# Five merges of one branch among the recurrence's chunks, none right behind its scores

## The chip, the cores and the metric

The kernel runs on one core of a Trainium2 chip. Its engines are TensorE (PE, with its weight loads as PEld), VectorE (DVE), ScalarE (ACT), GpSimd (POOL) and SyncE (SP, which issues the transfers). The metric is the device time of one execution in microseconds; lower is better.

## The reference

Two blocks on 256 tokens of width 1024. The first is a mixer and a mixture of experts; the second is two layers of feed-forward and attention. Only the mixer matters here:

```
proj = x @ w_in
y_a = rg_lru(...)                    # branch 0
y_b = gated_delta_rule(...)          # branch 1
y_c = stick_breaking_attention(...)  # branch 2
y_d = gla_chunked(...)               # branch 3
gates = sigmoid(merge_in)            # 4 x 1024 columns of proj
merged = sum over n of gates[:, :, n] * (y_n @ w_branch[n])
out = merged @ w_out
```

The recurrence of branch 3, with 16 chunks of 16 tokens and 4 heads:

```
attn = where(causal, q_dec @ k_inv.T, 0);  o_intra = attn @ v
def step(state, xs):
    o_i = q_i @ state
    state = state * gl_i[..., :, None] + kd_i.T @ v_i
    return state, o_i
```

## The kernel before

All four branches run on one core, and what stands in the list STEPS sets the order of the work on PE, ACT and DVE: each engine walks the same list and does its own part of each step. Weights come in units of 1 MB into a ring of six slots; SP requests a unit as soon as the slot that it needs is free.

A merge step ("merge", k) makes 128 of the 1024 output columns of one branch. PE does eight fp32 matmuls of 256 columns for the gate (xT times a unit of w_in) and four for the branch (yT times a unit of w_branch). In the trace each fp32 matmul is two instructions, so a merge reads as x16 and x8. ACT takes the sigmoid (sg), DVE multiplies and adds to merged (two operations of 0.42 us). There are 32: 0 to 7 for branch 0, 8 to 15 for branch 2 (the second in BRANCH_ORDER, attention), 16 to 23 for branch 3, 24 to 31 for branch 1. A merge needs only its branch's finished yT, a ring unit and one of two PSUM banks, so it can stand among steps of another branch. Merges 3, 7, 11 and so on free three ring slots.

The steps of branch 3 around the change:

- d_attn: PE makes the scores (gl_q, gl_k) and transposes d_kd. DVE masks the scores into d_at and makes two masked copies of the transposes, d_kn, 1.3 us each.
- d_intra: PE multiplies d_at with gl_v. It waits for both copies.
- d_chunk c: PE makes the chunk's update (d_kn times gl_v, four matmuls of 128 columns on 32 rows), DVE adds it to the decayed state in four operations (d_B in the trace), PE then reads out chunk c with the state that DVE wrote for the chunk before (gl_q with d_B, four matmuls of 16 columns).
- d_end: ACT squares the result, PE sums (d_e with ones, two matmuls of 512 columns), ACT makes the norm in two steps with table loads, DVE scales and gates into yT.
- b_rows: PE starts the next branch (rowbc with ones). It waits for DVE's yT of d_end.

_weave puts a list of merges evenly among a list of steps, the first one behind the first step. The waits on PE that matter, of d_chunk, d_intra and b_rows (comments mine):

```
pe.wait_ge(sem("d_S"), c)      # the read-out waits for DVE's state
t.see("d_am")                  # d_intra waits for the masked copies
pe.wait_ge(sem("y3"), 1)       # b_rows waits for yT of branch 3
```

Of the kernel before, what the change touches and what calls it, by code (L numbers as in the profile page):

```python
# [70 lines left out]
STEPS = [("proj", w, u) for w in "abcd" for u in range(PROJ_UNITS[w])]  # L71
# [19 lines left out]
def _weave(steps, tiles):  # L91
    out, put = [], 0
    for n, s in enumerate(steps):
        out.append(s)
        while put < len(tiles) and put * len(steps) < (n + 1) * len(tiles):
            out.append(tiles[put])
            put += 1
    return out + tiles[put:]


_MERGE = [("merge", k) for k in range(4 * DT)]
for hp in range(4):
    STEPS += [("c_z", hp), _MERGE[2 * hp], ("c_cum", hp), _MERGE[2 * hp + 1], ("c_out", hp)]
STEPS += [("d_gate",), ("b_pre",), _MERGE[8], _MERGE[9], ("d_attn",), _MERGE[10], ("d_intra",)]
STEPS += _weave([("d_chunk", c) for c in range(16)], _MERGE[11:14])
STEPS += [("d_end",), _MERGE[14], _MERGE[15], ("b_rows",), ("b_decay",), _MERGE[16], _MERGE[17], ("b_kk",), _MERGE[18],
          ("b_nat",), _MERGE[19]]
STEPS += _weave([(s, lv, half) for lv in range(1, 6) for s in ("b_y", "b_xy") for half in range(2)]
                + [("b_uw",)] + [(s, c) for c in range(4) for s in ("b_w", "b_o")] + [("b_end",)],
# [2520 lines left out]
```

## Time and profile before

| | us |
|---|---|
| median of 3 runs | 2322.02 |
| the three runs | 2322.02, 2322.64, 2316.07 |
| the profiled execution | 2322.17 |
| its span | 2320.4 |

The profiled execution's own time is 1.8 us above its span. Over the span PE is busy for 90%, DVE for 51%, ACT for 40%. The page's line of the granted clock gives TensorE's clock in tenths of full speed; its mean is 0.923. There are two levels, 1.00 (2.4 GHz) and 0.50 (1.2 GHz). The steps that the change touches lie between 330 and 430 us.

### The profile page before, as it was taken

The page shows a single profiled execution, that of the slowest core. Times are in us where ns is not written, and L with a number is a line of the kernel's source. Part 1 is how long each engine was busy: PE and PEld are TensorE (multiplying, and loading weights), DVE is VectorE, ACT ScalarE, POOL GpSimd, SP SyncE. Part 2 cuts the span into 40 slices and gives each one's busy share as a digit, 9 for nine tenths or more (in the row PEclk, how much of TensorE's full clock was granted, in tenths as well). Part 3 has the DMA queues.
Part 4 walks back from the last instruction along what each step waited for, and adds up shares of the span by engine and source line. Part 5 has one row for each costly group of instructions (what it writes and reads, how often), then busy time and mean ns, then how long its engine had stood idle before and what let it go on. Part 6 is the DMA issues. An engine that isn't in the chain of part 4 may idle for free.

```text
span 2320.4 us, 29178 instructions
## 1 busy us (share of the span) xinstructions
PE 2079.5 (90%) x11729; PEld 1722.8 (74%) x11729; DVE 1193.4 (51%) x1737; ACT 932.4 (40%) x1341; POOL 52.0 (2%) x126
## 2 busy tenths in 40 slices
PE   8999879989998999996899877879989998658998
PEld 6777668778467878775899752379989988536998
DVE  2060243441177878888555545455565555344554
ACT  1232530211045766675434523433354345344433
POOL 5000000000000000000000000000000000000000
PEclk9999886988989999998999998989999998759999
DMA  7775111203587888886365579335555555203553
GB/s 229 272 263 172 55 55 55 85 25 120 220 327 268 319 308 310 290 329 249 127 198 175 171 291 398 123 122 190 183 182 164 182 172 189 92 0 127 179 187 105
DMA packets 205351, 435.49 MB, mean 188 GB/s; under 512 B 7744, under 2 KB 158368, under 8 KB 181696
## 3 DMA queue, kind: packets, MB, share of 16 engines
q1 hardware_dynamic: 201568, 424.70, 52.7%
q0 software_dynamic: 3680, 9.37, 1.2%
q8 instruction: 70, 1.15, 0.2%
q14 instruction: 33, 0.27, 0.0%
HBM read 432.85 MB, written 1.20 MB: 187 GB/s over the span
## 4 chain that ended last, share of the span: by engine, by line
PE 62%; DVE 8%; ACT 5%; DMA 2%; issue 2%; DVEq 0%; ACTq 0%; SPq 0%
PE P L642 60%; ACT big L1419 2%; DMA ring<-in_ada_w 1%; DVE w_lo L2306 1%; DMA ring<-in_w_up 1%; DVE w_lo L1909 1%; ACT merged L1419 1%; DVE xs L1858 1%; PE P L1257 0%; PE P L658 0%; DVE big L1858 0%; DVE st L2494 0%; ACT xT L1419 0%; DVE xT L1854 0%; ACT w_hi L1455 0%
## 5 line engine op out<-in xcount | busy, mean ns | idle before, releaser
L1909 DVE TENSOR_TENSOR w_lo<-ring,w_hi 128x1024 fp32r<-128x1024 f32 x302 | 351.7, 1220 | 96.4 <-ACT w_hi L1455 96.2
L642 PE MATMUL P<-x_hi,w_hi 128*128 128x256 f32 x1280 | 362.9, 284 | 6.0 <-DVE w_lo L1909 6.0
L642 PE MATMUL P<-x_hi,w_lo 128*128 128x256 f32 x1280 | 363.5, 284 | 0.0
L642 PE MATMUL P<-x_lo,w_hi 128*128 128x256 f32 x1280 | 360.8, 282 | 0.0
L1455 ACT ACTIVATE w_hi<-ring 128x1024 fp32r<-128x1024 f32 x302 | 297.5, 1050 | 65.1 <-DMA ring<-in_ffn_w_down 62.3
L2306 DVE TENSOR_TENSOR w_lo<-ring,w_hi 128x1024 fp32r<-128x1024 f32 x240 | 279.2, 1221 | 22.1 <-ACT w_hi L1644 20.3
L642 PE MATMUL P<-w_hi,x_hi 128*128 128x256 f32 (+2 forms) x752 | 259.1, 345 | 24.9 <-DVE x_lo L1851 15.1
L1644 ACT ACTIVATE w_hi<-ring 128x1024 fp32r<-128x1024 f32 x240 | 240.4, 1053 | 100.6 <-DMA ring<-in_w_up 40.0
L642 PE MATMUL P<-xT,ring 128*128 128x256 f32 x1152 | 271.7, 394 | 3.1 <-ACT xT L1419 3.1
L642 PEld LDWEIGHTS P<-xT,ring 128*128 128x128 f32 x1152 | 225.9, 199 | 50.1 <-issue 18.1
L642 PE MATMUL P<-w_lo,x_hi 128*128 128x256 f32 (+2 forms) x752 | 256.8, 341 | 0.0
L642 PE MATMUL P<-w_hi,x_lo 128*128 128x256 f32 (+2 forms) x752 | 253.6, 337 | 0.0
L642 PEld LDWEIGHTS P<-x_hi,w_hi 128*128 128x128 f32 x1280 | 243.3, 190 | 10.0 <-DVE w_lo L1909 6.7
L642 PEld LDWEIGHTS P<-x_lo,w_hi 128*128 128x128 f32 x1280 | 244.9, 191 | 2.8
L642 PEld LDWEIGHTS P<-x_hi,w_lo 128*128 128x128 f32 x1280 | 244.3, 191 | 0.0
L642 PE MATMUL P<-w_hi,hid_hi 128*128 128x512 f32 x512 | 203.7, 398 | 4.7 <-DVE w_lo L2306 4.4
L642 PE MATMUL P<-w_lo,hid_hi 128*128 128x512 f32 x512 | 205.1, 401 | 0.0
L642 PE MATMUL P<-w_hi,hid_lo 128*128 128x512 f32 x512 | 201.5, 394 | 0.0
L1635 ACT ACTIVATE silu<-P 128x256 f32<-128x256 f32 x88 | 33.9, 385 | 372.9 <-PE P L642 356.4
L642 PEld LDWEIGHTS P<-w_hi,x_hi 128*128 128x128 f32 x752 | 149.9, 199 | 43.2 <-issue 19.7
L2286 DVE TENSOR_TENSOR hid<-silu,P 128x256 f32<-128x256 f32 (+1 forms) x80 | 33.7, 422 | 263.7 <-ACT silu L1635 263.1
L642 PEld LDWEIGHTS P<-w_hi,x_lo 128*128 128x128 f32 x752 | 149.2, 198 | 14.7
(437 smaller groups left out, 2472.0 us busy)
## 6 DMA issues: line engine op xcount, KB each, us to landing
ring<-in_ada_w SPq DMA_DIRECT2D x72, 1024.0 KB, 9.4
ring<-in_ffn_w_gate SPq DMA_DIRECT2D x44, 1024.0 KB, 5.5
ring<-in_ffn_w_up SPq DMA_DIRECT2D x44, 1024.0 KB, 7.9
ring<-in_ffn_w_down SPq DMA_DIRECT2D x44, 1024.0 KB, 4.9
ring<-in_w_in SPq DMA_DIRECT2D x40, 1024.0 KB, 7.4
ring<-in_w_gate SPq DMA_DIRECT2D x40, 1024.0 KB, 5.0
ring<-in_w_up SPq DMA_DIRECT2D x40, 1024.0 KB, 5.0
ring<-in_w_down SPq DMA_DIRECT2D x40, 1024.0 KB, 5.1
```

The costliest lines, as they stand in the source:

```text
L642: return pe.matmul(o, l, r, start=start, stop=stop, **kw)
L1419: a.done(act.activation(o, i, fn, **kw), name)
L1455: act.activation(w_hi[:, slot, c:c + half], ring[:, slot, c:c + half], ACT.Copy).then_inc(sem("w_hi"), 1)
L1635: act.activation(silu[:, k % 2, :], P[:, k % 2, 0:S], ACT.Silu).then_inc(sem("silu"), 1)
L1644: act.activation(w_hi[:, n % R, c:c + UNIT // 2], ring[:, n % R, c:c + UNIT // 2], ACT.Copy).then_inc(sem("w_hi"), 1)
L1858: v.done(dve.scalar_tensor_tensor(out=o, in0=x, scalar=s, in1=y, op0=op0, op1=op1), name)
L1909: dve.tensor_tensor(w_lo[:, slot, c:c + half], ring[:, slot, c:c + half], w_hi[:, slot, c:c + half].bitcast(F32), ALU.subtract).then_inc(s ...
L2286: dve.tensor_tensor(x, silu[done:128, k % 2, :], P[done:128, k % 2, S:2 * S], ALU.mult).then_inc(sem("hid_part"), 1)
L2306: dve.tensor_tensor(w_lo[:, n % R, c:c + UNIT // 2], ring[:, n % R, c:c + UNIT // 2], w_hi[:, n % R, c:c + UNIT // 2].bitcast(F32), ALU.su ...
```

## The change

Merge 10 no longer stands between d_attn and d_intra, and merge 14 no longer stands behind d_end. Both go into the recurrence, so that five merges (10 to 14) lie among its 16 chunks where there were three (11 to 13). Nothing else is changed.

```
-STEPS += [("d_gate",), ("b_pre",), _MERGE[8], _MERGE[9], ("d_attn",), _MERGE[10], ("d_intra",)]
-STEPS += _weave([("d_chunk", c) for c in range(16)], _MERGE[11:14])
-STEPS += [("d_end",), _MERGE[14], _MERGE[15], ("b_rows",), ("b_decay",), _MERGE[16], _MERGE[17], ("b_kk",), _MERGE[18],
+STEPS += [("d_gate",), ("b_pre",), _MERGE[8], _MERGE[9], ("d_attn",), ("d_intra",)]
+STEPS += _weave([("d_chunk", c) for c in range(16)], _MERGE[10:15])
+STEPS += [("d_end",), _MERGE[15], ("b_rows",), ("b_decay",), _MERGE[16], _MERGE[17], ("b_kk",), _MERGE[18],
```

On PE, from the scores on (L807 is the transpose, xT and yT with ring are the two halves of a merge, d_at with gl_v is d_intra, d_kn with gl_v is the update of chunk 0):

```order
 L642 MATMUL P<-gl_q,gl_k 128x128 x8
 L807 MATMUL P<-ident,d_kd 128x128 x8
-L642 MATMUL P<-xT,ring 128x256 x8
-L642 MATMUL P<-yT,ring 128x256 x4
 L642 MATMUL P<-d_at,gl_v 128x128 x8
 L642 MATMUL P<-gl_v,d_kn 128x128 x4
 L642 MATMUL P<-xT,ring 128x256 x8
 L642 MATMUL P<-yT,ring 128x256 x4
```

The merge between transposes and d_intra is gone; the merge behind chunk 0 stays in its place (it was merge 11 and is now merge 10).

On PE in the changed kernel, from the read-out of one chunk over a merge and three chunks to the next merge (gl_v with d_kn is a chunk's update, gl_q with d_B its read-out):

```order
L642 MATMUL P<-gl_q,d_B 128x16 x4
L642 MATMUL P<-xT,ring 128x256 x8
L642 MATMUL P<-yT,ring 128x256 x4
L642 MATMUL P<-gl_v,d_kn 128x128 x4
L642 MATMUL P<-gl_q,d_B 128x16 x4
L642 MATMUL P<-gl_v,d_kn 128x128 x4
L642 MATMUL P<-gl_q,d_B 128x16 x4
L642 MATMUL P<-gl_v,d_kn 128x128 x4
L642 MATMUL P<-gl_q,d_B 128x16 x4
L642 MATMUL P<-xT,ring 128x256 x8
L642 MATMUL P<-yT,ring 128x256 x4
```

Three chunks stand between two merges, where five stood before: the merges come behind chunks 0, 3, 6, 9 and 12, not 0, 5 and 10.

On PE at the end of the recurrence (d_e with ones are the sums of d_end):

```order
 L642 MATMUL P<-gl_v,d_kn 128x128 x4
 L642 MATMUL P<-gl_q,d_B 128x16 x8
 L642 MATMUL P<-d_e,ones 128x512 x2
-L642 MATMUL P<-xT,ring 128x256 x8
-L642 MATMUL P<-yT,ring 128x256 x4
 L642 MATMUL P<-xT,ring 128x256 x8
 L642 MATMUL P<-yT,ring 128x256 x4
```

One merge is left between the sums and b_rows. ACT's and DVE's parts of the merges move in the same way; POOL's and SP's lists are the same.

## Rows read from the trace of the kernel before

**Rows 1.** The page: busy time by engine, and one DMA row.
```profile
PE 2079.5 (90%) x11729; PEld 1722.8 (74%) x11729; DVE 1193.4 (51%) x1737; ACT 932.4 (40%) x1341; POOL 52.0 (2%) x126
...
ring<-in_w_in SPq DMA_DIRECT2D x40, 1024.0 KB, 7.4
```

**Rows 2.** Timeline, 330 to 343 us: start, length, engine, line, operation, operands, count.
```profile
333.60 1.91 PE L807 MATMUL P<-ident,d_kd 128*128 128x128 f32 x8
...
335.30 3.66 PE L642 MATMUL P<-xT,ring 128*128 128x256 f32 x16
335.62 2.60 DVE L1855 TENSOR_SCALAR d_kn<-P,parity 128x1024 f32<-128x1024 f32 x2
...
340.52 1.95 PE L642 MATMUL P<-d_at,gl_v 128*128 128x128 f32 x16
...
342.40 1.15 PE L642 MATMUL P<-gl_v,d_kn 32*128 32x128 f32 x8
```

**Rows 3.** Timeline, 343 to 364 us: first merge in the recurrence.
```profile
343.49 3.72 PE L642 MATMUL P<-xT,ring 128*128 128x256 f32 x16
...
348.86 1.15 PE L642 MATMUL P<-gl_v,d_kn 32*128 32x128 f32 x8
...
350.49 1.50 DVE L1858 SCALAR_TENSOR_TENSOR d_B<-d_B,d_gl,P 128x128 f32<-128x128 f32 x4
...
353.53 2.07 PE L642 MATMUL P<-gl_v,d_kn 32*128 32x128 f32 x8
...
357.35 2.07 PE L642 MATMUL P<-gl_v,d_kn 32*128 32x128 f32 x8
```

**Rows 4.** Timeline of PE, 364.85 to 409 us: second and third merge.
```profile
364.90 5.97 PE L642 MATMUL P<-xT,ring 128*128 128x256 f32 x16
...
372.53 1.15 PE L642 MATMUL P<-gl_v,d_kn 32*128 32x128 f32 x8
...
376.95 2.07 PE L642 MATMUL P<-gl_v,d_kn 32*128 32x128 f32 x8
...
388.32 6.20 PE L642 MATMUL P<-xT,ring 128*128 128x256 f32 x16
...
396.18 1.15 PE L642 MATMUL P<-gl_v,d_kn 32*128 32x128 f32 x8
...
400.37 2.07 PE L642 MATMUL P<-gl_v,d_kn 32*128 32x128 f32 x8
```

**Rows 5.** Windows, PE alone: stretch, length, busy (instructions), granted clock, DMA share, GB/s.
```profile
352.40:364.80 12.40, 12.40 (x55) 0.50 0.65 218
364.80:369.50 4.70, 4.70 (x13) 0.50 0.00 0
...
376.30:388.30 12.00, 12.00 (x53) 0.50 0.01 1
```

**Rows 6.** Timeline, 410 to 430 us: end of the recurrence.
```profile
410.97 3.41 PE L642 MATMUL P<-d_e,ones 128*128 128x512 f32 x4 [1.17 <-ACT d_e L1419]
...
414.22 3.62 PE L642 MATMUL P<-xT,ring 128*128 128x256 f32 x16
...
419.34 1.22 DVE L1851 TENSOR_TENSOR d_e<-d_e,P 128x1024 f32<-128x1024 f32 x1 [11.49 <-ACT d_e L1419]
...
420.60 1.28 DVE L1858 SCALAR_TENSOR_TENSOR yT<-d_e,cols,gate_d 128x1024 f32<-128x1024 f32 x1
...
424.58 3.60 PE L642 MATMUL P<-rowbc,ones 128*128 128x512 f32 x8
```

**Rows 7.** Timeline of PE, 454 to 475 us: two gaps, with their length in brackets.
```profile
459.42 1.16 PE L642 MATMUL P<-b_X,rowbc 128*128 128x128 f32 x8 [2.42 <-DVE rowbc L1851]
...
468.02 1.67 PE L642 MATMUL P<-b_X,rowbc 128*128 128x128 f32 x8 [2.26 <-DVEq L222]
```

**Rows 8.** Windows, PE alone: the same stretches.
```profile
457.00:465.00 8.00, 5.58 (x31) 1.00 0.76 258
468.50:471.90 3.40, 3.40 (x19) 0.50 0.02 8
```
## The prediction

> **What bounds the kernel now.** I read four views in this order: the page's busy times, the timeline around the moved merges, the windows with the granted clock, and the timeline again for the gaps further on. The page [rows 1] says that the tensor engine (PE) works for 90% of the span, so the question is always what PE does at a given place, and at which of its two clocks. The change touches about 95 us of 2320.
>
> Place one, behind the scores. The transposes end at 333.60 + 1.91 = 335.51. DVE then needs until 335.62 + 2.60 = 338.22 for the two masked copies (d_kn) that the intra step waits for. PE does not stand still, because merge 10 runs from 335.30 to 340.52, and the intra step follows at 340.52 [rows 2]. So merge 10 (5.2 us) covers a hole of some 2.8 us.
>
> Place two, the recurrence, from 342.40 [rows 2] to 410.97 - 1.17 = 409.80 [rows 6], with three merges in it. The reader would expect PE to wait for DVE there: each chunk's state update takes DVE 1.50 us and the next chunk's read needs it. The windows show otherwise: PE is busy all the time (12.40 of 12.40 us), but at half clock, 0.50, which is 1.2 GHz [rows 5]. A chunk takes 357.35 - 353.53 = 3.82 us at that clock [rows 3], while the first two behind a merge take 4.67 us together [rows 3], or 4.42 and 4.19 us [rows 4], so 2.1 us each at full clock. A merge that starts at full clock takes 348.86 - 343.49 = 5.37 us [rows 3]; one that starts at half clock takes 7.63 us (364.90 to 372.53) or 7.86 us (388.32 to 396.18) [rows 4]. What the engine did before the changes: the clock rose 4.7 us into a merge (at 369.5, of one that began at 364.8), and it was down again at 352.4 and 376.3, 3.5 and 3.8 us behind a merge's end, PE having been busy throughout with chunks [rows 3 to 5]. So merges raise the clock and chunks lose it, with a lag on both sides.
>
> Place three, behind the recurrence. The norm's sums start at 410.97; two merges follow from 414.22; b_rows starts at 424.58. b_rows needs yT of this branch, which DVE finishes at 420.60 + 1.28 = 421.88, 10.91 us behind the start of the sums [rows 6]. The two merges outlast that by 2.7 us, one merge would not.
>
> **The change part by part.** No instruction is added or removed on any engine, only rows move. The sum is made against the profiled execution, 2322.17 us.
>
> 1. Merge 10 leaves place one. The intra step then waits for DVE and starts at about 338.22 + 0.1 = 338.3 instead of 340.52: 2.2 us earlier. The merge's 5.2 us are not saved but paid inside the recurrence, so a hole of 2.8 us is uncovered. The intra step takes 342.40 - 340.52 = 1.88 us and chunk 0's first half 343.49 - 342.40 = 1.09 us [rows 2, 3], which ends at 341.3.
>
> 2. The recurrence now has merges behind chunks 0, 3, 6, 9 and 12. Merge 10 starts at full clock if that has held: 5.37, then two chunks 4.67, then the third at half clock 3.82, together 13.86 us, which gives 355.1. The next three groups start at half clock: a merge of 7.75 (mean of 7.63 and 7.86), two chunks of 4.30 (mean of 4.42 and 4.19), one of 3.82, together 15.87 us; three are 47.6, which gives 402.7. The last group has 7.75 + 4.30 and then only the reading half of chunk 15, a little under half of a slow chunk, 1.85: 13.9, which gives 416.6. Before it was 409.80: 6.8 us later. DVE's two small merge operations per merge come two times more, but behind a merge the update ran from 350.49 to 351.99 and the read that needs it, of chunk 2, follows PE's own work [rows 3]; I cost them at nothing. If they were not covered it would be under 1 us each.
>
> 3. Merge 14 leaves place three. The sums, ACT's steps and DVE's two steps stay as they are, so yT is ready 10.91 us behind the start of the sums and b_rows starts about 10.95 behind it, where it was 424.58 - 410.97 = 13.61 before: 2.65 us earlier. Merge 15 alone runs from 3.25 to 8.6 us behind the start, so a second hole of 2.3 us is uncovered in front of b_rows.
>
> 4. The holes can cost clock as well. Two gaps of PE of like length stand further on: 2.42 us before 459.42, with the clock at 1.00 all through, and 2.26 us before 468.02, with 0.50 from 468.5 to 471.9 [rows 7, 8]. So a fall is about an even matter, and it lasts 3.4 us, which costs half of that, 1.7. The bounds are 0 and 3.4 for the two holes together, and more if merge 10 begins at half clock, when it costs 7.75 instead of 5.37. I take 1.6.
>
> 5. Ring slots: merge 11's end frees three slots, and moves from about 349 to about 362. A transfer takes 7.4 us from its issue [rows 1], and the first reader is merge 16, behind b_rows, over 50 us later. No cost; the cover is the rest of the recurrence.
>
> Sum: 6.8 - 2.65 + 1.6 = +5.8 us, which makes 2328.0. The same from the other side: PE's work is the same, the two holes add 2.8 + 2.3 = 5.1 us of idle time, and the time at half clock stays nearly what it was, as five short slow stretches replace three long ones. The reason that more merges do not help is that three chunks at full clock last 6.2 us, longer than the 3.5 to 3.8 us after which the clock is gone. The median shown, 2322.02, is close to the profiled time, but one of the three runs is at 2316.07, so the moments at which the clock steps may well shift a run by several us.
>
> **Rivals.**
>
> *The clock holds* (faster). If three chunks between merges were few enough to keep 2.4 GHz, the recurrence would take 1.09 + 5 x 5.37 + 14 x 2.1 + 1.0 = 58.3 us from 340.2, ending at 398.5 instead of 409.8. With the sums at full clock (1.7 less) and place three's 2.65 that is 15.7 us less: 2306.5. Against it: both falls came within 4 us of a merge, with a busy PE [rows 4, 5]. The place that decides is the third chunk of each group.
> The Trainium skill, "TensorE: Matmul & The Clock Gate", section "What's actually happening", says that the clock is low by default and that activity releases it. If any busy PE counts as active, that page speaks for this rival. The trace disagrees with so plain a reading: PE was 12.00 of 12.00 us busy at 0.50 [rows 5].
>
> *The rises come early* (no change). The lag between a merge's start and the rise was 4.7 us, but nothing ties it to the merge. If the four later merges got their clock after about 2 us, each would cost some 1.3 us less: 5.8 - 5.2 = +0.6, so 2322.8. For it speaks that merges now follow the last rise more closely; against it, both merges seen at half clock cost almost the same [rows 4].
>
> *Both holes lose the clock* (slower still). PE stands for 2.8 us before the intra step, falls to 1.2 GHz, and intra, chunk 0 and merge 10's first part run at it: 1.9 + 1.1 us become twice as long and merge 10 takes 7.75, 5.4 us at most; b_rows adds 1.7. From the 4.2 of steps 1 to 3 that gives up to +11, and with the merge that follows recovering a part, about +9.5: 2331.7. The second gap of rows 7 speaks for it, the first against it.
>
> **How the numbers follow.** Forecast 0.45, clock holds 0.08, early rises 0.27, both holes 0.20. A measurement of this kernel can tell about 0.3%, that is 7 us, from no change. Faster by more comes only with the first rival: 0.08. Slower by more than 7 us (above 2329) takes the last rival, 0.20, and about a third of the forecast's own spread, which runs from 2324 to 2332: 0.36 in all. The rest, 0.56, is within 0.3%. The range reaches over the forecast and both rivals beside it, and down over half of the way to the first: 2315 to 2335.
>
> **What would show it.** In the changed trace: PE idle for about 2.8 us before the intra matmuls and about 2.3 us before b_rows; the clock at 0.50 in the third chunk of each group; the merges in the recurrence at 7.6 to 7.9 us but for the first; the recurrence's end 6 to 8 us later than 409.80, and merge 16's start 4 to 8 us later. Wrong would be: clock 1.00 across a whole group, merges of 5.4 us inside the recurrence, an intra step that waits for nothing, or a shift that is made up for later, for instance by a wait for a transfer that shrinks.

## The result and the profile after

| | before | after |
|---|---|---|
| median of 20 runs, us | 2316.64 | 2323.65 |
| lowest to highest, us | 2310.55 to 2322.64 | 2317.64 to 2328.83 |
| the profiled execution, us | 2322.17 | 2320.24 |
| its span, us | 2320.4 | 2318.5 |

The changed kernel is slower: the ratio of its runs to those of before is 1.0030, with a 95% interval of 1.0019 to 1.0041. Of 2316.64 us that is 7.0 us by the medians, and between 4.4 and 9.5 by the interval. The interval excludes 1, so the change is slower, but by hardly more than these runs can tell. The ratios here and below are worked out over the runs and can differ a little from the quotient of the two medians. One run of the kernel before in the second batch of experiments took 8225.72 us, counts as slow and is left out of the ratios.

The two profiled executions stand the other way round, 1.9 us apart. Each is one draw out of a spread of 11 to 12 us, so their spans do not compare the kernels. What can be compared is a stretch that starts and ends at the same instruction in both. I use the one from the start of the score matmuls (gl_q with gl_k) to the start of merge 16 (the first xT with ring behind b_rows): 330.02 to 429.62, 99.60 us, before; 324.61 to 429.69, 105.08 us, after. So within the traces the change costs 5.5 us, and what came before the scores had happened to be 5.4 us shorter.

The windows over the two stretches, before first (stretch, length, PE busy, granted clock, DMA share, GB/s), show where the 5.5 us are:

```profile
330.02:429.62 99.60, 98.43 (x453) 0.73 0.13 42
324.61:429.69 105.08, 99.62 (x453) 0.75 0.12 42
```

PE stands idle for 1.17 us before and for 5.46 us after, so 4.3 of the 5.5 us are idle time. The time at half clock, read in windows of 0.1 us, is 53.3 us before and 53.1 us after: two merges more among the chunks did not shorten it. The last 1.2 us are in PE's busy time and are not broken down further.

Place one in the changed kernel, in the timeline (start, length, engine, line, operation, operands, count; idle time before it in brackets). These rows answer to [rows 2]:

```profile
324.61 3.78 PE L642 MATMUL P<-gl_q,gl_k 128*128 128x128 f32 x16 [11.15 <-DVE gl_k L1851]
...
328.18 1.91 PE L807 MATMUL P<-ident,d_kd 128*128 128x128 f32 x8
...
330.20 2.60 DVE L1855 TENSOR_SCALAR d_kn<-P,parity 128x1024 f32<-128x1024 f32 x2
...
332.87 3.34 PE L642 MATMUL P<-d_at,gl_v 128*128 128x128 f32 x16 [2.77 <-DVE d_kn L1855]
...
336.14 1.46 PE L642 MATMUL P<-gl_v,d_kn 32*128 32x128 f32 x8
...
337.52 3.72 PE L642 MATMUL P<-xT,ring 128*128 128x256 f32 x16
```

PE stands for 2.77 us in front of the intra step, waiting for DVE's d_kn. The intra step then takes 336.14 - 332.87 = 3.27 us instead of 1.88. The clock was still at 1.00 through the idle time and fell at 333.4, 0.5 us into the step. From the scores' start to chunk 0's start it is 11.53 us where it was 342.40 - 330.02 = 12.38.

The recurrence, answering to [rows 3, 4]. Each pair is a merge's start and the start of the first chunk behind it; the rows of 2.07 us are third chunks:

```profile
342.90 1.15 PE L642 MATMUL P<-gl_v,d_kn 32*128 32x128 f32 x8
...
347.06 2.07 PE L642 MATMUL P<-gl_v,d_kn 32*128 32x128 f32 x8
...
350.79 5.21 PE L642 MATMUL P<-xT,ring 128*128 128x256 f32 x16
...
357.66 1.15 PE L642 MATMUL P<-gl_v,d_kn 32*128 32x128 f32 x8
...
362.71 2.07 PE L642 MATMUL P<-gl_v,d_kn 32*128 32x128 f32 x8
...
366.44 5.91 PE L642 MATMUL P<-xT,ring 128*128 128x256 f32 x16
...
374.01 1.15 PE L642 MATMUL P<-gl_v,d_kn 32*128 32x128 f32 x8
...
378.48 2.07 PE L642 MATMUL P<-gl_v,d_kn 32*128 32x128 f32 x8
...
382.21 6.55 PE L642 MATMUL P<-xT,ring 128*128 128x256 f32 x16
...
390.42 1.15 PE L642 MATMUL P<-gl_v,d_kn 32*128 32x128 f32 x8
...
398.10 5.45 PE L642 MATMUL P<-xT,ring 128*128 128x256 f32 x16
...
405.20 1.15 PE L642 MATMUL P<-gl_v,d_kn 32*128 32x128 f32 x8
```

The first merge takes 342.90 - 337.52 = 5.38 us, the others 6.87, 7.57, 8.21 and 7.10. The third chunks run at half clock (366.44 - 362.71 = 3.73). The windows show the clock, answering to [rows 5]:

```profile
333.50:336.70 3.20, 3.20 (x15) 0.50 0.00 0
350.80:353.70 2.90, 2.90 (x8) 0.50 0.00 0
366.40:370.80 4.40, 4.40 (x11) 0.50 0.57 181
382.20:387.90 5.70, 5.70 (x15) 0.50 0.00 0
```

The first is the intra step, the others are the first parts of merges 11, 12 and 13: PE is busy in all of them, at 1.2 GHz. The clock comes back 3.1 to 5.8 us into these merges. It is gone again by the start of the third chunk, in one group 0.2 us into it.

Place three, answering to [rows 6]:

```profile
413.14 3.78 PE L642 MATMUL P<-d_e,ones 128*128 128x512 f32 x4 [1.17 <-ACT d_e L1419]
...
416.71 4.61 PE L642 MATMUL P<-xT,ring 128*128 128x256 f32 x16
...
424.57 3.67 PE L642 MATMUL P<-rowbc,ones 128*128 128x512 f32 x8 [1.52 <-DVE yT L1858]
...
429.69 3.72 PE L642 MATMUL P<-xT,ring 128*128 128x256 f32 x16
```

The one merge left starts at half clock and takes longer, and b_rows waits another 1.52 us for yT. From the sums' start to merge 16's start it is 16.55 us, where it was 429.62 - 410.97 = 18.65.

### The profile page after: what moved, and what is told of

It reads as the page before. It is cut to its first block, busy times and chain, and to the rows that moved or that the text cites. A ratio compares the mean times of both kernels' runs of the same rounds, so it can differ in the third digit from the quotient of the medians.

```text
span 2318.5 us, 29178 instructions
## 1 busy us (share of the span) xinstructions
PE 2074.8 (89%) x11729; PEld 1719.0 (74%) x11729; DVE 1193.7 (51%) x1737; ACT 931.6 (40%) x1341; POOL 51.8 (2%) x126
## 4 chain that ended last, share of the span: by engine, by line
PE 62%; DVE 9%; ACT 5%; DMA 2%; issue 2%; DVEq 0%; ACTq 0%
PE P L642 60%; ACT big L1419 2%; DVE w_lo L2306 1%; DMA ring<-in_ada_w 1%; DMA ring<-in_w_up 1%; DVE w_lo L1909 1%; ACT merged L1419 1%; DVE xs L1858 1%; PE P L658 0%; PE P L1257 0%; DVE big L1858 0%; DVE st L2494 0%; ACT xT L1419 0%; DVE xT L1854 0%; ACT w_hi L1455 0%
## 5 line engine op out<-in xcount | busy, mean ns | idle before, releaser
L642 PE MATMUL P<-w_hi,x_hi 128*128 128x256 f32 (+2 forms) x752 | 260.2, 346 | 25.1 <-DVE x_lo L1851 15.1
```

Source lines behind the costliest of these rows:

```text
L642: return pe.matmul(o, l, r, start=start, stop=stop, **kw)
```

## The experiments

Every stretch below is read from one profiled execution. By my estimate it carries an error of 1 to 2 us from where the clock's steps fell: the same piece of work behind the recurrence took 18.65 us in one trace and 20.24 in another. Each kernel has 6 to 12 runs, against 11 to 33 runs of the kernel before in the same batch (medians 2318.47, 2319.36 and 2318.97 in the three batches). "The stretch" is from the scores to merge 16, 99.60 us before and 105.08 with the change. In the expectations, theory A is the prediction's account (idle time is uncovered, the time at half clock stays); rival B is another one, named anew for each kernel. "Recurrence" is from chunk 0's start to the end of the last read-out, which is 1.17 us in front of the sums.

**Each half of the change alone.**

```
# e1_first: merge 10 moved, 14 and 15 at the end
STEPS += [..., _MERGE[8], _MERGE[9], ("d_attn",), ("d_intra",)]
STEPS += _weave([("d_chunk", c) for c in range(16)], _MERGE[10:14])
STEPS += [("d_end",), _MERGE[14], _MERGE[15], ("b_rows",), ...]
# e2_second: merge 14 moved, 10 behind the scores
STEPS += [..., ("d_attn",), _MERGE[10], ("d_intra",)]
STEPS += _weave([("d_chunk", c) for c in range(16)], _MERGE[11:15])
STEPS += [("d_end",), _MERGE[15], ("b_rows",), ...]
```

> Only merge 10 is moved (from behind the scores into the recurrence, four merges there); merges 14 and 15 stay at the end. Measure: the stretch from the start of the score matmuls to the start of merge 16, 99.6 us before and 105.1 with the whole change. Theory A (two uncovered holes, time at half clock about conserved): the hole of 2.8 us in front of the intra step is there, b_rows has none; the stretch is 102 to 104 us, the median 2 to 5 us above before. Rival B (the loss comes from merges that start at half clock in the recurrence, not from the holes): the loss goes with the number of merges added there, so half of it, about 2.7 us, with the clock steady across the hole.

> Only merge 14 is moved (from behind the recurrence into it, four merges there); merge 10 stays behind the scores. Theory A: no hole in front of the intra step, one of 1.5 to 2.7 us in front of b_rows; stretch 101 to 102.5 us, median 1 to 3 us above before, less than with merge 10 moved alone. Rival B: the same 2.7 us as for merge 10 alone.

Measured: e1_first 2324.46 us, ratio 1.0017 (1.0002 to 1.0032); e2_second 2324.03 us, ratio 1.0021 (1.0002 to 1.0040). Both are slower, and their medians do not tell them apart. The medians are 6.0 and 5.6 us above before, more than the 2 to 5 and 1 to 3 us expected; the ratios make it 3.9 and 4.9 us, with intervals that reach down to 0.5 us. PE's timeline of e1_first (the starts of scores, intra step, chunk 0, sums, merge 14 and merge 16):

```profile
322.86 3.79 PE L642 MATMUL P<-gl_q,gl_k 128*128 128x128 f32 x16 [11.15 <-DVE gl_k L1851]
...
331.12 3.31 PE L642 MATMUL P<-d_at,gl_v 128*128 128x128 f32 x16 [2.77 <-DVE d_kn L1855]
334.36 1.48 PE L642 MATMUL P<-gl_v,d_kn 32*128 32x128 f32 x8
...
407.46 3.78 PE L642 MATMUL P<-d_e,ones 128*128 128x512 f32 x4 [1.17 <-ACT d_e L1419]
411.03 4.88 PE L642 MATMUL P<-xT,ring 128*128 128x256 f32 x16
...
427.70 3.72 PE L642 MATMUL P<-xT,ring 128*128 128x256 f32 x16
```

and of e2_second (scores, chunk 0, sums, b_rows, merge 16):

```profile
326.64 3.78 PE L642 MATMUL P<-gl_q,gl_k 128*128 128x128 f32 x16 [11.14 <-DVE gl_k L1851]
...
339.01 1.15 PE L642 MATMUL P<-gl_v,d_kn 32*128 32x128 f32 x8
...
411.91 3.78 PE L642 MATMUL P<-d_e,ones 128*128 128x512 f32 x4 [1.17 <-ACT d_e L1419]
...
423.34 3.67 PE L642 MATMUL P<-rowbc,ones 128*128 128x512 f32 x8 [1.60 <-DVE yT L1858]
...
428.45 3.72 PE L642 MATMUL P<-xT,ring 128*128 128x256 f32 x16
```

With merge 10 gone the same hole of 2.77 us and the same slow intra step are there; with merge 10 in its place the chunks begin 12.37 us behind the scores, as before. The recurrence takes 71.9 us (334.36 to 407.46 - 1.17) and 71.7 us with four merges. The stretches are 104.84 and 101.81 us. The second is as theory A had it, the first 0.8 us above its range. In the first, rival B has the clock steady across the hole, and it was not. The second, 2.2 us longer than before, does not tell A from B, which said 2.7.

The two losses, 5.2 and 2.2 us, make 7.4 together where the whole change has 5.5. Part of this is place three of e1_first: its merge 14 began at half clock (merge 15 at full), so it took 427.70 - 407.46 = 20.24 us against 18.65, for the same work. The clock came back 2.9 us behind the start of the sums in the trace of before, and 6.1 us behind it in this one. It came back 5.1 to 5.7 us behind it in after, e2_second, e3_fill, e4_block, e6_split3 and e8_none, and 3.3 in e7_early. So the trace of before is a favourable draw at this place. That moving merge 10 costs more than moving merge 14 is seen in these traces and not settled by the medians.

**The holes filled.**

```
+ for _ in range(5):      # before the wait of d_intra; 3 before that of b_rows
+     mm(P[:, 2, 0:S], xT[:, 0, 0:128], xT[:, 0, :])
```

> The changed kernel with extra matmuls of 256 columns on a free PSUM bank in both holes, five in front of the intra step and three in front of b_rows; their results are overwritten and no work is left out. They take no time that was not idle. Theory A: the clock stays at 1.00 through both holes, so intra and chunk 0 take 3.0 us as before instead of 4.65, and the stretch is 103 to 104 us where the change has 105.1: the idle time itself is not given back. If the holes cost nothing but clock, the stretch would be near 100.

Measured: 2324.97 us, ratio 1.0022 (1.0004 to 1.0040), not told from the changed kernel's 1.0030. Its trace:

```profile
330.44 3.79 PE L642 MATMUL P<-gl_q,gl_k 128*128 128x128 f32 x16 [11.15 <-DVE gl_k L1855]
...
338.70 2.05 PE L642 MATMUL P<-d_at,gl_v 128*128 128x128 f32 x16 [0.60 <-DVE d_kn L1859]
340.68 1.15 PE L642 MATMUL P<-gl_v,d_kn 32*128 32x128 f32 x8
...
416.03 3.78 PE L642 MATMUL P<-d_e,ones 128*128 128x512 f32 x4 [1.17 <-ACT d_e L1423]
...
427.37 3.70 PE L642 MATMUL P<-rowbc,ones 128*128 128x512 f32 x8 [0.35 <-DVE yT L1862]
...
432.52 3.72 PE L642 MATMUL P<-xT,ring 128*128 128x256 f32 x16
```

The intra step takes 340.68 - 338.70 = 1.98 us again, at full clock, and the scores' start to chunk 0's start 10.24 us instead of 11.53. The stretch is 102.1 us, 0.9 under what theory A gave and 2.1 above the 100 that it would be if the holes cost nothing but clock. At the hole 1.3 us came back, and 0.3 more in chunk 0's first half (341.77 - 340.68 = 1.09 us instead of 1.38), so the first fall is worth 1.6 us. The remaining 1.4 us of the gain lie in the rest of the recurrence, where nothing was filled and the clock's steps fell otherwise. What stays, 102.1 - 99.6 = 2.5 us, is not the clock in the holes. The medians show no gain from the filling.

**Five merges in one block.**

```
-STEPS += _weave([("d_chunk", c) for c in range(16)], _MERGE[10:15])
+STEPS += [("d_chunk", 0)] + _MERGE[10:15] + [("d_chunk", c) for c in range(1, 16)]
```

> The changed kernel with the same five merges in one block behind chunk 0, not spread. Theory A with the prices of the trace: five merges at full clock 26.9, two chunks at full clock, twelve at 3.82 us: the recurrence ends about 80 us behind chunk 0's start against 75.8 in the changed kernel, so the stretch is about 109 us and the median about 4 us above the changed kernel. Rival B (starting at half clock is what costs): no merge starts at half clock here, so the stretch is shorter than 105.1, by up to 4 times 2.3 us.

Measured: 2330.12 us, ratio 1.0043 (1.0023 to 1.0064); stretch 108.6 us, as theory A had it. The ratio is 3 us above the changed kernel's, from another batch; 4 were expected. Rival B falls: here no merge starts at half clock, and the recurrence is longer.

```profile
324.11 3.78 PE L642 MATMUL P<-gl_q,gl_k 128*128 128x128 f32 x16 [11.14 <-DVE gl_k L1851]
...
335.58 1.52 PE L642 MATMUL P<-gl_v,d_kn 32*128 32x128 f32 x8
...
416.19 3.78 PE L642 MATMUL P<-d_e,ones 128*128 128x512 f32 x4 [1.17 <-ACT d_e L1419]
...
432.74 3.72 PE L642 MATMUL P<-xT,ring 128*128 128x256 f32 x16
```

The recurrence takes 415.02 - 335.58 = 79.4 us against 75.8 with the same merges spread. A merge that starts at half clock costs about 2.4 us more, and the two chunks behind it together take some 3.3 us less.

**No merge in the recurrence.** The kernel before, with

```
+STEPS += [("d_chunk", c) for c in range(16)]
+STEPS += [("d_end",), _MERGE[11], _MERGE[12], _MERGE[13], _MERGE[14], _MERGE[15], ("b_rows",), ...]
```

> The kernel before with no merge in the recurrence: 11, 12 and 13 stand with 14 and 15 behind its end, 10 behind the scores. Measures what a merge inside costs. Theory A, from the prices of the trace: 1.1 + 4.2 + 12 slow chunks of 3.82 + 1.9 = 53 us for the recurrence where before has 67.4, so 4.8 us net for each of three merges, against 5.2 us for each of them behind the end at full clock: stretch from the scores to merge 16 about 101 us against 99.6, the median within 3 us of before. Rival B: if merges inside really warmed up what follows them, taking them out would cost clearly more, 5 us and up.

Measured: 2324.51 us, ratio 1.0022 (1.0010 to 1.0035), 5.2 us above before and so 2 us more than I had allowed; stretch 103.4 us where I gave 101. By its median it is just where rival B began (5 us and up), by its stretch, 3.8 us longer, it is not. The window over most of its chunks, from 340 us on:

```profile
340.00:390.00 50.00, 48.83 (x207) 0.50 0.00 1
```

The chunks alone run at 0.50 with PE always busy, since the missing 1.17 us is the wait in front of the sums. The recurrence takes 54.3 us. With 0, 3, 4, 4 and 5 whole merges it takes 54.3, 67.4, 71.9, 71.7 and 75.8, so each adds 4.3 to 4.4 us, less than the 5.4 that it lasts at full clock. Two more kernels give 3.7 (e7_early below, two merges, 61.7) and 4.0 (e3_fill, five, 74.2). The miss of some 2.5 us has two equal parts: the recurrence took 54.3 us instead of 53, and the part behind it grew by 16.9 us for three merges instead of 15.6, as the first began slowly.

**The same merges in small pieces.** The question left was whether a finer mix keeps the clock. "Small pieces" means that PE's part of a merge is cut into its twelve matmuls; ACT's and DVE's part stands behind the last of them:

```
+for n, s in enumerate(_chunks):              # e5_split5: merges 10 to 14, 60 matmuls
+    STEPS.append(s)
+    for p in _mm[n * len(_mm) // 15:(n + 1) * len(_mm) // 15]:
+        STEPS.append(p)                      # one matmul on PE
+        if p[2] == 11:
+            STEPS.append(_MERGE[p[1]])       # ACT's and DVE's part of the merge
```

e6_split3 does this to the kernel before and its merges 11 to 13.

> The changed kernel with its five merges cut into their twelve matmuls on PE, four of them behind each of the chunks 0 to 14 (ACT's and DVE's part stands behind the last matmul of a merge). Same work, same place, other grain. Theory A (chunks lose the clock because PE sees little but their small matmuls for several us, and the merges regain it late): a chunk with four matmuls of 256 columns takes 2.1 + 1.8 = 3.9 us at a clock that stays at 1.00, so the recurrence, from chunk 0's start to the squares, takes 58 to 62 us where the changed kernel has 75.8, and the median falls by 12 to 17 us under the changed kernel. Rival B (any chunk drags the clock down, whatever is between): at half clock it takes 3.8 + 3.6 = 7.4 us per chunk, and the recurrence over 100 us.

> The kernel before with its three merges of the recurrence cut up in the same way, two or three matmuls behind each of the chunks 0 to 14; merges 10 and 14 in their old places. Theory A: 2.1 + 1.1 = 3.2 us per chunk if the clock holds, so the recurrence takes 48 to 51 us where before has 67.4, and the median falls by 12 to 18 us. If so few matmuls are not enough to hold the clock: 3.8 + 2.1 = 5.9 us per chunk at half clock, 90 us.

Measured: e5_split5 2307.47 us, ratio 0.9957 (0.9942 to 0.9973); e6_split3 2331.61 us, ratio 1.0053 (1.0035 to 1.0071). PE's timeline in e5_split5, of one chunk's update, its four matmuls and the next update, and the window over the recurrence but for its first 0.8 us:

```profile
348.31 1.15 PE L656 MATMUL P<-gl_v,d_kn 32*128 32x128 f32 x8
...
350.31 1.97 PE L656 MATMUL P<-xT,ring 128*128 128x256 f32 x8
352.21 1.15 PE L656 MATMUL P<-gl_v,d_kn 32*128 32x128 f32 x8
```

```profile
338.00:396.70 58.70, 57.99 (x358) 1.00 0.16 54
```

A chunk and its four matmuls take 352.21 - 348.31 = 3.90 us, the sum of 2.1 and 1.8 that theory A gave, at a clock of 1.00 from 338 us to the end. The recurrence takes 58.8 us instead of 75.8 with the very same instructions. The window of e6_split3 over its recurrence:

```profile
342.70:421.60 78.90, 78.90 (x313) 0.59 0.12 40
```

Here the mean clock is 0.59 and the recurrence takes 78.9 us, 11.5 more than with the same three merges whole. Two or three matmuls a chunk did not hold the clock: it fell at 349.4 and came back only twice, for 3.4 us each time. Theory A's 48 to 51 us and a fall of 12 to 18 us were a clear miss, since the median rose by 12.3; the 90 us for a clock that does not hold was nearer.

**Merges in earlier holes.** On the kernel before, the gate step is cut in two on ACT and DVE:

```
+STEPS += [("d_gate",), _MERGE[8], _MERGE[9], ("d_gate2",), ("b_pre",), _MERGE[10], ("d_attn",), _MERGE[11], ("d_intra",)]
+STEPS += _weave([("d_chunk", c) for c in range(16)], _MERGE[12:14])
```

> The kernel before with the gate step of branch 3 cut in two on ACT and DVE, merges 8 and 9 between the halves there, merge 10 in front of the scores on PE (where PE stood for 11.15 us), merge 11 in the hole behind the scores, and only merges 12 and 13 in the recurrence; 14 and 15 at the end as before. Theory A (a merge costs what its place leaves uncovered; one in the recurrence costs about 4.2 us net, one in a hole little): from merge 8's start to merge 16's start 121.4 us before, here 114 to 118; the median 4 to 7 us under before. Rival B (what counts is the number of merges that start at half clock): merge 10 starts at half clock in place of one in the recurrence, so no gain.

Measured: 2310.37 us, ratio 0.9967 (0.9953 to 0.9981), 9.0 us under before by the medians and 7.7 by the ratio, somewhat more than the 4 to 7 expected.

```profile
319.84 6.18 PE L642 MATMUL P<-xT,ring 128*128 128x256 f32 x16 [4.60 <-DVE merged L1853]
...
327.59 1.95 PE L642 MATMUL P<-gl_q,gl_k 128*128 128x128 f32 x16
...
337.31 1.15 PE L642 MATMUL P<-gl_v,d_kn 32*128 32x128 f32 x8
```

Merge 10 starts as soon as DVE has added merge 8, between the two halves of its gate step, and the idle time in front of it is 4.60 us where 11.15 us stood in front of the scores. It takes 327.59 - 319.84 = 7.75 us, mostly at half clock, but the scores then run at full clock. From merge 8's start to merge 16's start the trace has 114.3 us against 121.4 before. What counts is what a merge covers; rival B, which gave no gain, falls.

**Both together.** The merges in the recurrence are cut up in all three; there are four of them.

```
e9_early_split4:        8, 9 in the gate step; 10 before the scores; 11-14 cut; 15 at the end
e10_early_hole_split4:  8, 9 in the gate step; 10 before, 11 behind the scores; 12-15 cut; none at the end
e11_hole_split4:        8, 9 before, 10 behind the scores; 11-14 cut; 15 at the end
```

> The two gains together: merges 8 and 9 between the halves of the gate step on ACT and DVE, merge 10 in front of the scores, merges 11 to 14 cut up among chunks 0 to 14 (three or four matmuls behind each), 15 at the end. Open is whether 3.2 matmuls a chunk hold the clock: 4 did, 2.4 did not. If they do: the recurrence takes 52 to 55 us and merge 8's start to merge 16's start about 101 to 104 us (108.0 with five cut merges, 121.4 before), the median 16 to 20 us under before. If they do not: chunks of 6 to 7 us for a part, recurrence 65 to 85 us.

> As the kernel before it in this batch, but merge 11 covers the hole behind the scores and 12 to 15 are cut up in the recurrence, so that none is left at the end and b_rows waits for yT: 7 us uncovered there instead of 2.3, against 2.2 covered at the intra step. Theory A: some 2 us worse than with merge 15 at the end, and the clock is lost at the end.

> The kernel before with merge 10 in its old place and merges 11 to 14 cut up in the recurrence (what e2_second does with whole merges), 15 at the end; the gate step as before. Shows grain alone at four merges: with whole merges the recurrence took 71.7 us. If 3.2 matmuls a chunk hold the clock: 52 to 55 us, and the median 14 to 18 us under before. If not: 65 to 85 us, and slower than before.

Measured: 2303.89 us (ratio 0.9942, 0.9921 to 0.9963), 2301.39 (0.9918, 0.9900 to 0.9937) and 2302.78 (0.9923, 0.9902 to 0.9943). All three are faster than both kernels, by 15 to 18 us against the one before, and their intervals overlap. For e9_early_split4 I had expected 16 to 20 us, and its median gives 15.1. The window over e11_hole_split4's recurrence:

```profile
336.80:390.00 53.20, 53.20 (x337) 1.00 0.19 60
```

Three or four matmuls a chunk did hold the clock: 53.3 us in place of 71.7 in e2_second, which has the same merges whole at the same places. From merge 8's start to merge 16's start the three have 103.9, 104.6 and 105.1 us. The order of e9 and e10 that I expected is in the traces (0.7 us instead of 2) and not in the medians, so it stays open. The early merge brought little on top of the cut. All three have four merges in the recurrence. e9_early_split4 covers part of the wait in front of the scores and leaves the hole behind them bare (4.06 us); e11_hole_split4 does it the other way round, and the traces are 1.2 us apart. e10_early_hole_split4 covers both and pays with 7.65 us in front of b_rows.

## Why the prediction was right

The forecast was +5.8 us; the traces have +5.5 and the medians +7.0. As a time it was 2328.0, and the median is 2323.65: it was added to a profiled execution that stood 5.5 us above the later median of before, and so came out 4.4 us too high. The mechanism was right, idle time uncovered at both places with the time at half clock unchanged (53.3 and 53.1 us). By its steps:

| step | forecast | the traces |
|---|---|---|
| 1. merge 10 out, hole of 2.8 us, without loss of clock | -2.2 | -0.85, with a hole of 2.77 us |
| 4. clock lost in the holes | +1.6 | 1.6 in the first (1.3 contained in the row above, 0.3 in the row below), none in the second |
| 2. recurrence, from chunk 0's start (the text's 6.8 is this less the 2.2 of step 1) | 76.4 - 67.4 = +9.0 | 75.8 - 67.4 = +8.4 |
| 3. merge 14 out | -2.65 | -2.1 |
| sum | +5.8 | +5.5 |

That the sum is off by 0.3 us only is partly luck. Step 2 was 0.6 too large and step 3 0.55 too small, which cancels, and the trace of before was a favourable draw at place three: with e1_first's 20.24 us there instead of 18.65 the difference would be 3.9 us.

Step 1 was right. Step 4 was right in its total, but it called each fall an even matter. The first hole, 2.77 us long, lost the clock in all four kernels that have it without filling (after, e1_first, e4_block and e5_split5, each with an intra step of 3.2 to 3.3 us), and so did the 4.06 us of e9_early_split4. The second kept it in five (after, e2_second, e4_block, e5_split5 and e9_early_split4, where b_rows' start to merge 16's start takes 5.1 us, against 5.04 before) and lost it in e11_hole_split4, where the same takes 6.82, and in e10_early_hole_split4 with its 7.65 us. The gap was 2.47 us in e5_split5, which kept the clock, and in e11_hole_split4, which lost it, so its length alone does not decide. e3_fill shows the first fall's price by taking it away.

Step 2 carried the sum and was right by its mechanism: chunks lose the clock (3.0 to 4.4 us behind a merge in this trace), merges bring it back late. The slow merges came out at 7.4 us in the mean instead of 7.75, with 6.87 and 8.21 outside the 7.6 to 7.9 that was to show it, and the first two chunks behind them at 4.2 to 5.1 instead of 4.3. The premise that the clock is gone 3.5 to 3.8 us behind a merge was narrower than the spread: over all traces with whole merges in the recurrence it is 2.8 us (e7_early) to 5.8 (e3_fill), so that three chunks of 6.2 us in all are nearly held in the best case. One merge more inside costs 4.3 us, as five kernels agree, 3.7 to 4.4 with all seven.

Step 3 promised 0.55 us more than was given back. I had let the sums and merge 15 run at full clock; they ran and began at half clock, so yT came later, and the hole was 1.52 us long instead of 2.3.

Step 5 cost nothing: PE waited for no ring unit.

Of the rivals, "the clock holds" did not happen, as the windows show. Its place, the third chunk, was the right one to look at, and its price was about right too: e5_split5, in which it does hold, has a recurrence of 58.8 us where I had worked out 58.3. The Trainium skill, "TensorE: Matmul & The Clock Gate", section "What's actually happening", says that activity releases the throttle. Read so plainly that any busy PE counts as active, e8_none refutes it: 48.83 of 50.00 us busy, at 0.50. "The rises come early" happened in part: the four later merges took 6.87 to 8.21 us, in all 1.2 us less than forecast, where that rival has 5.2. "Both holes lose the clock" had the first hole only, and merge 10 began at full clock behind it (5.38 us).

The chance of 0.56 for "within 0.3%" against 0.36 for "slower" was a fair call for a change that came out at 0.30%.

## What to carry to other kernels

A place for movable work is worth what it covers: look up how long the engine would stand there without it, at both places, before moving. On PE look at the granted clock beside the busy time, since a stretch that is 100% busy with small matmuls can run at half clock; there the mix counts more than the amount. Large matmuls that are spread evenly, four behind each small group, gave 17 us here, which five blocks among the same groups did not. Too thin a spread, two or three behind each, was worse than whole merges: a recurrence of 78.9 us against 67.4.

## What the runs showed of the hardware

- TensorE's clock fell with PE busy throughout, 2.8 to 5.8 us behind the end of a merge, when only the chunks' matmuls (128 columns on 32 rows, and 16 columns) ran. I had read that from the trace; that it is so for 50 us on end (e8_none, 0.50) was new.
- The same instructions in another order ran at 1.00 for 58 us (e5_split5). With three or four large matmuls a chunk it was 1.00 over 53.2 us as well (e11_hole_split4), with two or three 0.59 in the mean (e6_split3). What exactly the chip counts was not measured.
- The clock can fall after a short stand of PE: a gap of 2.77 us was followed by a fall in four traces of four, one of 2.47 us in one of two, gaps of 1.5 to 2.0 us in none of four.
- The spread between runs of one kernel, 8 to 21 us, is mostly larger than the effect that was looked for.
